# Two transformer blocks in one program: the second block's last recall softmax moved beside the first dilated group, and its tiles dealt 4, 2, 2

## The reference, cut to what matters

```python
def memory_branch(mq, gate, mem_n, w_mem_kv):
    mk, mv = split_cols(mem_n @ w_mem_kv, [MEM_W, MEM_W])
    ...
    s = jnp.einsum('bshd,bmhd->bhsm', q, k).astype(jnp.float32) * (MEM_DH ** -0.5)
    p = jax.nn.softmax(s, axis=-1)
    o = jnp.einsum('bhsm,bmhd->bshd', p.astype(v.dtype), v).reshape(B, S, MEM_W)
    return o * jax.nn.silu(gate)

def dilated_layer(x, g, w_in, w_mem_kv, w_out, mem_n, kv):
    h = rmsnorm_2(x, g)
    ...
    for gi, (window, dil) in enumerate(DIL_CONFIG):
        o, lse = dilated_group(q, kv[2 * gi], kv[2 * gi + 1], dil, window // dil)
    ...
    o_mem = memory_branch(mq, gate_m, mem_n, w_mem_kv)
    return x + jnp.concatenate([o_dil, o_mem], axis=-1) @ w_out
```

## Time and profile before

| | us |
|---|---|
| median of 3 runs | 3854.31 |
| profiled execution, its own time | 3859.5 |
| span of its records | 3857.5 |
| PE busy | 3679.9 (95%) |
| PEld busy | 3200.8 (83%) |
| DVE busy | 1940.4 (50%) |
| ACT busy | 1651.6 (43%) |
| POOL busy | 1387.5 (36%) |
| PE on the chain that ended last | 79% |

### The profile page before, as it was taken

How to read it: one execution, slowest core, us unless ns; L and a number is a source line. 1 busy time by engine, 2 the same in 40 slices (tenths; PEclk the granted TensorE clock), 3 DMA queues, 4 the chain that set the end, 5 groups by cost and what they waited for, 6 DMA issues and landing times.

```text
span 3857.5 us, 72287 instructions
## 1 busy us (share of the span) xinstructions
PE 3679.9 (95%) x30708; PEld 3200.8 (83%) x30708; DVE 1940.4 (50%) x2454; ACT 1651.6 (43%) x2132; POOL 1387.5 (36%) x631
## 2 busy tenths in 40 slices
PE   8999999899989999999999999999899999999998
PEld 6777888777778888888878888987788888888887
DVE  3247887656555883444445444345333334343343
ACT  3442236544444443444444445444344444444443
POOL 2332222000023554454534454443343434433442
PEclk9999999999999999999999999999999999999999
DMA  8876774000025776655545554454555555555553
GB/s 299 303 263 230 280 273 151 25 4 4 22 76 182 236 264 190 195 189 187 193 150 177 171 180 162 164 164 158 187 175 175 170 175 174 171 178 175 171 170 125
DMA packets 183375, 668.91 MB, mean 173 GB/s; under 512 B 20464, under 2 KB 20464, under 8 KB 182416
## 3 DMA queue, kind: packets, MB, share of 16 engines
q1 hardware_dynamic: 176688, 643.12, 50.7%
q10 hardware_dynamic: 5088, 16.98, 1.2%
q0 software_dynamic: 1280, 4.20, 0.3%
HBM read 655.82 MB, written 8.39 MB: 172 GB/s over the span
## 4 chain that ended last, share of the span: by engine, by line
PE 79%; DVE 10%; ACT 5%; issue 2%; DMA 2%; PEld 2%; POOL 1%; ACTq 0%; PEldq 0%; SPq 0%; DVEq 0%; POOLq 0%
PE ps L1076 65%; DVE whl L2102 3%; ACT whl L1586 2%; DVE raw L2186 2%; PEld ps L1076 1%; PE ps L1330 1%; DMA raw<-in_mem 1%; PE ps L1316 1%; ACT work L1586 1%; PE ps L1307 1%; PE ps L1574 1%; PE ps L1558 1%; DVE tm L2105 1%; PE ps L1001 1%; PE ps L1023 1%
## 5 line engine op out<-in xcount | busy, mean ns | idle before, releaser
L1076 PE MATMUL ps<-halves,whl 128*128 128x256 f32 (+1 forms) x14752 | 2583.5, 335 | 74.8 <-DVE halves L2102 23.6
L1076 PEld LDWEIGHTS ps<-halves,whl 128*128 128x128 f32 x14752 | 2244.6, 191 | 381.0 <-issue 78.3
L2715 POOL TENSOR_TENSOR whl<-raw,whl 128x1024 fp32r<-128x1024 f32 x508 | 1259.2, 2479 | 1801.1 <-ACT whl L1586 1800.7
L1586 ACT ACTIVATE whl<-raw 128x1024 fp32r<-128x1024 f32 x1016 | 1056.4, 1053 | 969.5 <-PE ps L1076 676.0
L2102 DVE TENSOR_TENSOR whl<-raw,whl 128x1024 fp32r<-128x1024 f32 x508 | 808.8, 1593 | 1153.3 <-ACT whl L1586 1153.1
L1076 PE MATMUL ps<-whl,halves 128*128 128x256 f32 x2752 | 486.5, 336 | 4.6 <-ACT whl L1586 4.5
L1076 PEld LDWEIGHTS ps<-whl,halves 128*128 128x128 f32 x2752 | 418.6, 189 | 62.6 <-ACT whl L1586 5.5
L2186 DVE SCALAR_TENSOR_TENSOR raw<-raw,mix 128x1024 f32<-128x1024 f32 x128 | 240.1, 1903 | 4.5 <-DMA raw<-in_adaT 4.5
L1586 ACT ACTIVATE work<-ps 128x512 f32<-128x512 f32 (+1 forms) x208 | 119.0, 575 | 286.1 <-PE ps L1076 232.1
L2715 POOL TENSOR_TENSOR halves<-mix,halves 128x256 fp32r<-128x256 f32 (+1 forms) x15 | 25.0, 1682 | 410.8 <-ACT halves L1586 410.8
L2102 DVE TENSOR_TENSOR work<-work,ps 128x512 f32<-128x512 f32 x157 | 107.4, 684 | 109.9 <-ACT work L1586 109.1
(11 more groups left out here) (266 smaller groups left out, 2369.8 us busy)
## 6 DMA issues: line engine op xcount, KB each, us to landing
raw<-in_ffn SPq DMA_DIRECT2D x264, 512.0 KB, 4.3
raw<-in_w_kv SPq DMA_DIRECT2D x192, 512.0 KB, 3.7
raw<-in_w_in_b SPq DMA_DIRECT2D x160, 512.0 KB, 3.4
raw<-in_adaT SPq DMA_DIRECT2D x128, 512.0 KB, 5.3
raw<-in_w_in_a SPq DMA_DIRECT2D x128, 512.0 KB, 3.7
raw<-in_ada SPq DMA_DIRECT2D x64, 512.0 KB, 5.9
raw<-in_mem SPq DMA_DIRECT2D x64, 512.0 KB, 4.9
raw<-in_w_out_a SPq DMA_DIRECT2D x48, 512.0 KB, 3.5
```

The source lines that it names most:

```text
L1076: p = self.e.matmul(o, x, y, start=bi not in begun, stop=final and kc == 3 and m == len(pairs) - 1, skip_group_check=True)
L1586: return self.e.activation(out, in_, func, **kw)
L2715: return self.e.tensor_tensor(out, a, b, op)
```

## The change

`MEMORY_TURNS = (2, 4, 2, 2)` deals the recall groups of the second layer: two steps (the recalls), S, four tiles, T, two tiles, O, two tiles. The norm for the keys and values gives one column behind each step of a group, recalls included, where it gave one behind every two. Head 7 is no longer run out ahead of the fence: its generator goes to `pipeline_tight`, which deals it with `LAST_MEMORY_TURNS = (1, 4, 2, 2)` between the first 28 tiles of the first dilated group: E1, S, E2 to E5, T, E6 and E7, O. The wait for the store of x moves behind these 28 tiles, into `memory_done`, with waits for head 7's end. So that the buffers of these 28 tiles don't meet those that head 7 still uses, the ring of the dilated stage starts at buffer 6, and head 7 names its own ring `w2`.

```diff
+MEMORY_TURNS = (2, 4, 2, 2)
+LAST_MEMORY_TURNS = (1, 4, 2, 2)
...
-        rest(self.pipeline(self.memory_groups(1, "w_in_b", 32), 2, self.normed(5, 6, "HA"), self.normed(6, 6, "HB")))
+        last = self.pipeline(self.memory_groups(1, "w_in_b", 32), MEMORY_TURNS, self.normed(5, 6, "HA"), self.normed(6, 6, "HB"))
         self.f8 = self.fence()
         self.begin_dilated()
-        heads = self.pipeline_tight(self.dilated_groups())
+        heads = self.pipeline_tight(self.dilated_groups(), last)
...
+            elif ratio == MEMORY_TURNS:
+                weave(self.after(chain(*[g for _, g in made]), later, (1,)), heads, ratio)
             else:
                 run_all((chain(*[g for _, g in made]), ratio), (heads, 1), (limited(later, 6), 1))
...
-    def pipeline_tight(self, groups):
+    def pipeline_tight(self, groups, last):
...
             if before is None:
-                rest(part(made))
+                weave(part(made[:7]), last, LAST_MEMORY_TURNS)
+                self.memory_done()
+                rest(part(made[7:]))
...
     def dilated_groups(self):
-        self.m2 = 0
+        self.m2 = 6
...
     def mem_head(self, h, mk, mv, mq, mg, ch):
-        k, v, q = (self.ring[m % len(self.ring)] for m in (mk, mv, mq))
+        k, v, q = (self.w2[m % len(self.w2)] for m in (mk, mv, mq))
...
         self.e.dma_start(self.phc[:, 0:1152], self.io["dil_c"]).then_inc(self.sig("ld_dil", 0, 16), 16)
+
+    def memory_done(self):
+        self.wait_ge("mh_mm", (7, "o"))
+        self.wait_ge("mh_v", (7, "mix"))
         self.wait_ge("st_x", 0)
```

More of the change, by code:

```diff
@@ L616 @@
     ev_shift2 = ev_kA = ev_vA = ev_q = rotate_q = ev_r = ev_gd = ev_mem = ev_x = glu_gate = swiglu = nothing
-    reload_x = reload_x2 = begin_retention = begin_dilated = end = nothing
+    reload_x = reload_x2 = begin_retention = begin_dilated = memory_done = end = nothing
     normed = attn = no_steps
@@ L2644, in mem_head @@
         self.heads_begun += 1
-        p, g = self.big[slot], self.ring[mg % len(self.ring)]
+        p, g = self.big[slot], self.w2[mg % len(self.w2)]
         k = 8 * (h % 8)
```

## The result

The changed kernel takes 3830.09 us, the median of 4 runs (3823.22 to 3832.43), against 3853.56 of the kernel before beside it (4 runs, 3846.75 to 3855.78). The ratio is 0.9936, 95% interval 0.9922 to 0.9950: faster by 24.7 us, of 19 to 30. The sum gave 17.7. The profiled execution took 3829.78 (span 3827.8, granted clock 0.985), 29.7 less than the one of before. A ratio with its interval is worked out over all launches, so it isn't exactly the quotient of the two medians beside it.

A forecast was written before the change was run, and what follows sets the result against it. PE, busy 95% of the span, was taken as the bound, gains being its idle or lower-clock moments; 4.7 + 13.0 = 17.7 us, less the profiled run's 5.2 over the median, gave 3836.6 us, range 3833 to 3840, over rivals 3829 to 3844.

The forecast's parts named there:

- The sum: Whole change: 4.7 us from the dealing plus 13.0 from head 7 and the fence, 17.7 us gained.
- The dealing, B, C and D: Recall groups: B loses 0.4, C gains 0.0 as a 3.9 us wait moves to C4, D gains 5.1; 4.7 us together.
- Rounds with two columns: ACT and DVE rounds beside B and C: two norm columns instead of one, 5.4 to 5.5 us against 5.39.
- rival 2: Groups B and C: rounds with two columns cost as those with four, 1.24 us more each; gain 12, 3842.5; chance 0.12.
- rival 4: Groups B and C: each norm column costs a round of its own; 30 us slower, 3885; chance 0.05.
- Where C4's lateness comes from: ACT and DVE queues: four rounds of 5.39 plus evictions, tanh, copies and exponentials make a chain of about 31.5 us.
- Head 7 and the fence: From head 7's scores to E4: 13.3 us lost, less 0.3 for the fence, 13.0 us gained.
- The store's collision: At the fence: store collides with loads or splits behind its issue are late, up to 7.6 us; gain 10, 3844; chance 0.07.
- Rival 1: Groups C and D: the wait doesn't move to C4, 10.6 + 13.0 = 23.6 us gained, 3830.7; chance 0.16.
- I take the same difference off both: Whole kernel: profiled execution 5.2 us above the median before, so 3841.8 profiled becomes 3836.6 in the median.
- the fence's loss: Head 7's scores to E4: 13.3 us of 25.32 lost, including 5.72 before T, 0.26 fence, 3.30 before E4.

The follow-up runs named there:

- norm_six: Changed kernel with the norm's columns dealt 0,1,0,1,0,1,0,1,1,1 over a group's ten steps, six per group; stage 143.3 us, ratio 0.9960 to the kernel before.
- norm_v3: Changed kernel with the norm's columns dealt 0,0,1,1,1,1,1,1,0,0 over a group's ten steps; stage 137.0 us, ratio 0.9930 to the kernel before, again 0.9935.
- norm_v2: Changed kernel with the norm's columns dealt 0,0,2,2,1,1,1,1,0,0 over a group's ten steps; stage 140.6 us, ratio 0.9937 to the kernel before.
- move_only: Changed kernel with the recall groups dealt as before, so only head 7 and the store's wait moved; ratio 0.9965 to the kernel before, 3839.83 us.
- ring6: Kernel before with only the dilated ring's start moved from buffer 0 to 6; ratio 0.9998 to the kernel before.
- turns_only: Changed kernel with head 7 and the store's wait in front of the fence as before, dealing and dense norm kept; ratio 0.9985, 3847.22 us.
- after_again: The changed kernel run again unaltered; ratio 0.9949 to the kernel before, 3832.49 us against 3851.46.
- store_wait_late: Kernel before with only ACT's wait for the store of x moved behind the first 28 dilated tiles; ratio 0.9985, 3849.82 us.

## Why the prediction was right or wrong, point by point

**The dealing, B, C and D: right, and in size.** The periods are 27.0, 31.0 and, to the fence, 26.3, where 26.6, 31.65 and 26.2 were said. The wait did move to C4, ended by POOL's low half: 3.02 us for 3.9, and 1.59 for 1.55 by the clock. With the 6.0 us by which this execution was ahead taken off, C4's high half was due at 2641.0 and came at 2640.6.

**Rounds with two columns: right.** They took 5.42 us, from the high half at 2622.87 to its like two tiles on, with two columns between them, where one column gave 5.39:

```profile
2622.87 1.06 ACT L1593 ACTIVATE whl<-raw 128x1024 fp32r<-128x1024 f32 x1
...
2628.29 1.04 ACT L1593 ACTIVATE whl<-raw 128x1024 fp32r<-128x1024 f32 x1
```

So the lock between DVE and POOL, which the Trainium skill states (page "SBUF — State Buffer", section "SBUF: two separate sides") and the low halves show, did not make the round longer: rival 2 falls, and rival 4 with it.

**Where C4's lateness comes from: half right.** I put it down to the chain of all rounds, evictions and softmax together, and said that a round takes about the same with one column or two; before `norm_six` I took from it that thinning the norm would not help. What a round takes was right. But `norm_v3` runs the same sixteen columns in the same stage without a wait. The chain as a whole is therefore shorter than PE's work; it comes out late where a column stands behind the last tiles or ahead of the softmax, and where two share a step (`norm_v2`, 1.48 us). Calling the chain the bound was wrong, though the wait that it gave was right by 0.9 us.

**Head 7 and the fence: right.** 13.2 us in `move_only`, for 13.0. The store's collision cost nothing.

**Rival 1** gives the measured time, 3830.7, and is not what happened: the wait it does without is in the trace, 4.6 us with its clock.

**The step that failed** is the last: "I take the same difference off both". The sum had no term for work that the change doesn't touch, and gave no reason for putting it at nothing; the fence's loss was read from one execution too. The stage gave 18.5 for 17.7, but three comparisons of the whole kernel give 0.9936, 0.9949 and 0.9945, 20 to 25 us, 21.8 on average. The runs show these in place of the missing term:

- Ahead of the stage the same instructions took 2587.2 to 2596.7 us in different executions, with no order by kernel; that is chance, and was 6.1 of the 29.7 us between the two profiled executions.
- Behind the stage PE has two cadences, below. The four traces with the old dealing took 1077.9 to 1079.9 there, the three of the changed kernel 1074.7, 1077.8 and 1074.8, on average 3.0 less.
- In the stage the kernel's old waits took 161.2 us in one execution and 163.4 in another (`ring6`), by the clock behind E4, so the gain there is 18.5 to 20.7.

Together the last two give 21.5 to 23.7 us, and the 21.8 of the launches lies within; the 24.7 of the first four launches is the highest of the three comparisons. Whether the dealing makes the faster cadence likelier stays open. The faster one came in eight of ten traces with the new dealing and in none of four with the old (by chance alone such a split would come in 1.5% of cases), and one program showed both. The ratio of `turns_only`, 5.8 us (1.9 to 9.6), does not settle it: its stage's 7.4 and 3 more would be just too much, but where the clock falls behind C4, as in all three traces of the changed kernel, the stage gives some 5.3, and 8.3 is inside. My range of 15 us took in the doubts about the stage and 1.5 us for the median; the three medians of the changed kernel lie 2.4 us apart.

## What to carry to other kernels

When a wait is taken away by more work ahead of it, ask which instruction of the late queue PE meets next, and work out its time too: here the gain in group C was 0.7 us of 5.5, because the fourth tile's split was as late as the transposes. Filler that several engines must hand to each other (multiply on one, copy on the next, subtract on the third) belongs in the middle of a stretch, not between the last tile and the softmax: dealing the same sixteen columns otherwise was worth 5.7 us in the stage, though the launches don't settle what it is worth in the whole. And before a forecast is set against a median, look at how much the parts of the program that aren't changed differ between executions.

## What the runs showed of the hardware

**Two cadences of one instruction stream.** At full granted clock and without idle time a tile of sixteen matmuls takes 2.773 us in one cadence and 2.82 to 2.83 in the other. From start to start, the 512-column matmul and the 256-column one take 230 and 116 or 117 ns, or 241 and 120, 235 and 114, 232 and 118 in turn. The slower executions have it only in stretches: cut into sixteens, the 5350 matmuls from the 24800th on are 334 pieces, of which 56 took about 0.05 us more in `after_again` than in the first trace of the changed kernel, and 256 the same to 0.01. A dilated group, 704 matmuls, takes 118.54 to 118.66 us, or 118.85 to 119.13. The same program had the first in two executions and the second in a third. In the ten tiles compared, the other engines' starts relative to PE's are the same in both to 0.1 us, which is what the cadence itself adds up to there. What sets it was not found: not the buffers' addresses (`ring6`), and not the idle time before E4 (`move_only` has none and the slower cadence, `turns_only` has 3.34 us and the faster).

**Whether the clock falls behind a short wait differs between executions.** In the three traces of the changed kernel idle times of 3.02, 3.16 and 3.09 us before C4 were followed by the half clock; one of 3.10 us at the same place in `turns_only` was not, and 2.74 in `norm_six` was (C4 took 4.16 us there). Before E4 it is alike: 3.30 us in the kernel before was not, 3.34 in `turns_only` and 2.96 in `ring6` were.

**A DMA issue can hold ACT.** The issue of the masks, right behind that of the 2 MB store, took 0.45 to 0.47 us in twelve of the fourteen traces, 0.62 in `norm_six` and 2.32 in `store_wait_late`. Why is not shown.
